# Slab 5 into the bank of the mean square, the first gate slab into bank 6, and the last query slab's mean, root and norm at other places

## The reference, cut to what matters

```
h    = RMSNorm(x)
proj = h @ w_in            # qa ka va | qb kb vb | gate_a gate_b
q, k = per-head RMSNorm    # 16 query heads, 8 + 2 key heads, width 64
ya   = block-sparse causal attention (8 heads); yb = sliding window 128 with sinks (8 heads, 2 kv heads)
x    = x + (sigmoid(gate_a) * (ya @ w_branch_a) + sigmoid(gate_b) * (yb @ w_branch_b)) @ w_out
x    = x + relu(RMSNorm(x) @ w1)^2 @ w2
```

## Time and profile before

| | us |
|---|---|
| median of 3 runs | 678.22 (678.0 to 679.57) |
| profiled execution | 676.66 |
| its span, first to last instruction | 674.9 |
| PE busy / weight loads | 668.8 / 553.7 |
| DVE / ACT / POOL busy | 504.8 / 370.2 / 322.9 |

### The profile page before, as it was taken

One profiled execution on the slowest core, in us unless ns is written; L12 is line 12 of the kernel. 1 busy time (PEld: TensorE's weight loads), 2 busy tenths in 40 slices (PEclk: granted clock), 3 DMA queues, 4 the chain that ended last, 5 costly groups with the idle time before them and its releaser, 6 DMA issues.

```text
span 674.9 us, 9472 instructions
## 1 busy us (share of the span) xinstructions
PE 668.8 (99%) x3238; PEld 553.7 (82%) x3238; DVE 504.8 (75%) x701; ACT 370.2 (55%) x662; POOL 322.9 (48%) x194
## 2 busy tenths in 40 slices
PE   9999999999999999999999999999999999999998
PEld 7878787788888888888888888888888888888886
DVE  6667898555555555785559879788797888978897
ACT  7467676676665566543347546254463525536360
POOL 0246676456556653444446436246352454435532
PEclk9999999999999999999999999999999999999999
DMA  8222242222232213555222232414132151220303
GB/s 320 95 93 94 76 128 82 78 81 93 96 94 75 71 45 113 157 181 188 82 93 93 100 118 65 153 62 154 64 113 104 62 186 62 93 101 25 125 0 125
DMA packets 22909, 69.87 MB, mean 104 GB/s; under 512 B 2731, under 2 KB 4011, under 8 KB 22876
## 3 DMA queue, kind: packets, MB, share of 16 engines
q1 hardware_dynamic: 22588, 68.92, 30.3%
q10 hardware_dynamic: 288, 0.52, 0.2%
HBM read 67.27 MB, written 2.16 MB: 103 GB/s over the span
## 4 chain that ended last, share of the span: by engine, by line
PE 94%; DVE 2%; ACT 2%; issue 1%; DMA 1%; POOL 0%; SPq 0%; DVEq 0%; ACTq 0%
PE bank L1375 20%; PE bank L1377 20%; PE bank L1376 20%; PE bank L1692 8%; PE bank L1689 8%; PE bank L1691 8%; PE bank L1476 3%; PE bank L1538 2%; PE bank L1525 2%; PE bank L1559 1%; PE bank L1561 1%; DMA store<-x_t 1%; PE bank L1661 1%; DVE store L1010 0%; PE bank L1404 0%
## 5 line engine op out<-in xcount | busy, mean ns | idle before, releaser
L534 POOL TENSOR_TENSOR w_lo<-w_raw,w_hi 128x1024 fp32r<-128x1024 f32 x77 | 190.2, 2474 | 232.7 <-ACT w_hi L624 232.7
L1375 PE MATMUL bank<-qk_hi,w_hi 128*128 128x512 f32 x320 | 125.0, 391 | 0.0
L1377 PE MATMUL bank<-qk_hi,w_lo 128*128 128x512 f32 x320 | 124.5, 389 | 0.0
L1376 PE MATMUL bank<-qk_lo,w_hi 128*128 128x512 f32 x320 | 124.5, 389 | 0.0
L1375 PE MATMUL bank<-x_hi,w_hi 128*128 128x512 f32 x304 | 122.4, 403 | 1.6 <-DVE v_parts L1016 1.1
L1377 PE MATMUL bank<-x_hi,w_lo 128*128 128x512 f32 x304 | 118.8, 391 | 0.0
L1376 PE MATMUL bank<-x_lo,w_hi 128*128 128x512 f32 x304 | 118.4, 389 | 0.0
L624 ACT ACTIVATE w_hi<-w_raw 128x1024 fp32r<-128x1024 f32 x80 | 83.9, 1056 | 59.4 <-PE bank L1377 55.0
L1258 DVE SCALAR_TENSOR_TENSOR store<-bank,softmax,store 128x512 f32<-128x512 f32 x101 | 72.0, 744 | 23.2 <-PE bank L1692 23.1
L1692 PE MATMUL bank<-v_parts,x_lo 128*128 128x512 f32 (+1 forms) x218 | 84.4, 387 | 0.0
L1689 PE MATMUL bank<-v_parts,x_hi 128*128 128x512 f32 (+1 forms) x218 | 84.4, 387 | 0.0
(11 more groups left out here) (165 smaller groups left out, 1213.1 us busy)
## 6 DMA issues: line engine op xcount, KB each, us to landing
w_raw<-slabs SPq DMA_DIRECT2D x80, 512.0 KB, 3.3
bias_m<-slabs SPq DMA_DIRECT2D x16, 512.0 KB, 3.6
qk_hi_again<-slabs SPq DMA_DIRECT2D x16, 512.0 KB, 5.2
store<-x_t SPq DMA_DIRECT2D x16, 256.0 KB, 3.4
bias_m<-tab_dram SPq DMA_DIRECT2D x8, 256.0 KB, 4.3
out<-store SPq DMA_DIRECT2D x7, 256.0 KB, 2.1
bias_m<-tab_dram SPq DMA_DIRECT2D x8, 128.0 KB, 3.6
w_raw<-slabs ACTq DMA_DIRECT2D x2, 256.0 KB, 3.4
```

The costliest lines, as they stand in the source:

```text
L534: pool.tensor_tensor(w_lo[:, g % WS, :], w_raw[:, g % RAW, :], w_hi[:, g % WS, :].bitcast(F32), ALU.subtract).then_inc(w_lo_ready, 1)
L1375: pe.matmul(out_, wh, xh, start=first, stop=False)
L1376: pe.matmul(out_, wh, xl, start=False, stop=False)
L1377: last = pe.matmul(out_, wl, xh, start=False, stop=end)
```

## The change: two banks, and the order of the last query slab's norm

- `acc(5)` becomes bank 5, which was the mean square's; PE's wait before slab 5 is `ms_ready` in place of the read of slab 0. Slab 10, in bank 0, now waits for slab 0's read, and the first table product (bank 5) for slab 5's.
- The first gate slab goes to bank 6 and waits for slab 13's read; the second, in bank 0, waits for slab 15's. The transposes of unit 1, which use bank 6, wait for the first gate scale.
- The head sum of slab 16 stands behind kt 5 of slab 17 instead of kt 6.
- On DVE the mean of slab 16 stands ahead of the norm of slab 15 instead of behind it; the norm of slab 16 stands behind the maxima of step 0 instead of in step 2 behind the reciprocals of step 1.
- On ACT the root of slab 16 stands ahead of the split of slab 19 instead of at the end of step 1.

```diff
         def acc(g):
-            return bank[(0, 1, 2, 6, 7)[g % 5]]
+            return bank[5 if g == N_VA + 1 else (0, 1, 2, 6, 7)[g % 5]]
+
+        def gate_bank(j):
+            return bank[0 if j else 6]
...
             for g in range(N_VA, N_QKV):
+                if g == LAST_V:
+                    qkv_root(LAST_Q)
                 split_hi(g + 2)
...
                 if 0 < step < STEPS:
                     exps(step)
-                if step == 1:
-                    qkv_root(LAST_Q)
...
                 else:
                     v_scale(g)
+                if g == LAST_Q:
+                    qk_mean(g)
                 if N_VA <= g - 1 < LAST_Q:
                     qk_norm(g - 1)
-                if not is_v(g):
+                if g < LAST_Q:
                     qk_mean(g)
...
-                dve.tensor_tensor(store[:, j, :], bank[0][:, :], r_all[:, :],
+                dve.tensor_tensor(store[:, j, :], gate_bank(j)[:, :], r_all[:, :],
                                   ALU.mult).then_inc(acc_read, 1)
...
-                if step == 2:
-                    qk_norm(LAST_Q)
                 for e in range(2):
                     if step >= 2:
                         probs_t_lo(*units(step - 2)[e])
                     if step < STEPS:
                         scores_max(*units(step)[e])
+                    if step == 0 and e == 1:
+                        qk_norm(LAST_Q)
...
                     pe.wait_ge(tabw_lo_ready, 1)
-                    pe.wait_ge(ms_ready, 1)
+                    qkv_read(N_VA + 1)
...
-            AFTER[LAST_V, 6] = LAST_Q
+            AFTER[LAST_V, 5] = LAST_Q
             for g in range(N_VA, N_QKV):
                 pe.wait_ge(w_lo_ready, g)
-                if g >= 5:
-                    qkv_read(g - 5)
+                if g == N_VA + 1:
+                    pe.wait_ge(ms_ready, 1)
+                elif g > N_VA + 1:
+                    qkv_read(0 if g == 10 else g - 5)
...
                         pe.wait_ge(pt_lo_ready, u - 1)
+                    if u == 1:
+                        pe.wait_ge(acc_read, read(G_GATE))
...
-                    if j:
+                    if j > 1:
                         pe.wait_ge(acc_read, read(g - 1))
                     else:
-                        qkv_read(g - 3)
-                last = slab_part(g, bank[0], from_x, kts, kts[0] == 0, stop)
+                        qkv_read(LAST_Q - 1 if j else LAST_Q - 3)
+                last = slab_part(g, gate_bank(j), from_x, kts, kts[0] == 0, stop)
```

## The result

| | before | after |
|---|---|---|
| median of 22 runs each | 677.18 us (676.07 to 679.57) | 679.28 us (677.02 to 682.41) |
| profiled execution's span | 674.9 us | 677.0 us |
| mean granted clock in it | 1.000 | 0.997 |

The ratio is 1.0032, 95% interval 1.002 to 1.0044: slower by 2.1 us, just past the 0.3% that a measurement tells from no change. The median of before over 22 runs is 1.0 us lower than that of the three runs that the forecast was built on.

A forecast was written before the change was run, and what follows sets the result against it. TensorE bounds the kernel, busy 668.8 of 674.9 us. Terms -0.54 -0.45 +2.69 -0.49 give +1.2 us: profiled 677.9, and 1.56 above that a median of 679.4 us; 8-in-10 range 677.1 to 680.9.

The forecast's parts named there:

- Slab 5: Slab 5 in bank 5 no longer waits for line 1016: gain 0.54 of 1.28 us, 0.74 returning at line 1403.
- Head sum, mean, maxima: Last query slab's head sum one kt sooner costs 0 to 0.1 us; mean before slab 15's norm costs nothing, maxima at 115.97.
- The gate slab: First gate slab in bank 6 waits for slab 13, not slab 15's norm: gain 0.45 us (0.3 to 0.5).
- The root on ACT and what it drags on POOL: Earlier root delays slab 19's split 1.15 us, itself hidden; POOL's line 534 moves to 116.38, 542 ends at 118.75.
- the race: POOL's line 534 starts 0.48 us ahead of DVE's 984; had POOL lost, v_lo at 122.9 and sum +0.7.
- The norm on DVE: Norm behind step 0's maxima waits for POOL's 534 and 542 in turn; v_lo_ready at 123.40, PE's new stall 2.69 us.
- the first rival: DVE's follow-up 987 goes ahead of POOL's queued 542: stall 1.71 us, sum +0.2, 678.4 us; chance 0.17.
- The gap: PE's new stall before step 2's scores, waiting for v_split_lo: 2.69 us, bounds 0 and 3.4.
- The second rival: Norm instructions cost only their median or lone times: no stall, sum -1.5, 676.7 us, or stall 0.6, sum -0.9; chance 0.12.
- The third stall: PE's second transposes, kept back at line 1111 by the norm in step 2, no longer wait: gain 0.49 us (0 to 0.5).
- The sum: Total of the terms, -0.54 -0.45 +2.69 -0.49 = +1.2 us; profiled execution 677.9 us, median 679.4 us.
- the third rival: PE's gap before step 2's scores sets the granted clock back: 1.3 us more, sum +2.5, 680.7 us; chance 0.11.

The follow-up runs named there:

- e2: The change with POOL's low part of slab 15 moved behind the normalising of step 0: 676.59 us against 677.41 for the kernel before, ratio 0.9994.
- e3: The change with POOL's low parts of slabs 19 and 15 both moved behind the normalising of step 0: 676.55 us against 677.41 before, ratio 0.9985.
- e9: The change with POOL's low part of slab 19 computed twice, one behind the other: 682.13 us against 677.36 for the kernel before, ratio 1.0063.
- e0: The changed kernel itself timed again beside the experiments, its profiled execution at full clock: 679.15 us against 677.41 for the kernel before, ratio 1.0028.
- e4: Both bank changes alone, with mean, root and norm of slab 16 as before: 676.64 us against 677.44 for the kernel before, ratio 0.9987.
- e5: Mean, root and norm at their new places, both banks as before: 679.47 us against 677.44 for the kernel before, ratio 1.0029.

## Why the prediction was right or wrong

**Slab 5** was right: 0.5 us of new idle at line 1403 (1409 now), on the squares' low part, as named, and a gain of 0.56 us where 0.54 was forecast.

**Head sum, mean, maxima**: right. No wait at the sum; the maxima of step 0 came at 114.94 and 115.34 with the norm of slab 15 short (0.69 and 0.69).

**The gate slab**: right in mechanism, too large in size. It starts 0.20 us after the last scores and waits for nothing, but the gain is 0.28 to 0.29 us instead of 0.45, just outside the bounds of 0.3 to 0.5.

**The root on ACT and what it drags on POOL**: right. ACT's split let POOL's 538 start 0.41 us ahead of line 988, where 0.48 was forecast; the race was not lost.

**The norm on DVE**: right in mechanism and size. Forecast were 2.5 and 1.7 us for its first two instructions; 2.54 and 1.67 were measured. The order POOL, DVE, POOL, DVE, which the 0.85 us of the earlier trace rows had suggested and on which the first rival hung, held. The gap was forecast at 2.69 us of PE's order and is 2.48. Of the 0.21, 0.04 lie in the way from line 1046 to PE, for which the earlier trace rows gave 2.32+0.15 and the trace after 2.22+0.21; some 0.15 lie in PE's arrival, later by what the gate slab gained less. The gate slab's error and this one nearly cancel each other in the sum. e2, e3 and e9 take away one POOL instruction, both, or add one, and the norm follows each time. The second rival is refuted by the trace after; e3 shows the condition that it needed, a POOL at rest, with 0.69 us for each. The Trainium skill ("SBUF — State Buffer", section "Who interferes with whom") has the rule that such instructions shut each other out whole and don't share. Every one of these rows agrees: 0.54 to 0.55 us after POOL's end, each time.

**The third stall**: right. The transposes of step 3 wait for nothing; from the scores of step 2 to the late split, e0 is 0.59 us quicker than before, where 0.49 was forecast.

**The sum** was +1.2 us. Between the traces of before and e0, at full clock in both, it is +1.04 (-0.55 -0.29 +2.48 -0.59). The medians of the executions at full clock can't confirm it so closely: 0.3 us over before in the 22 runs, 1.2 in e0. The change as it is came out at +2.1, and the step that failed is the weight of the third rival: I gave the fall of the clock 0.11, since the trace had only a gap of 1.28 us to show. It came in 19 of 34 executions. Its price was about right: 1.3 us forecast from a stretch as long as the gap, 1.6 between the traces with and without the fall (the stretch is longer, some 3.4 us). With forecast and rival at about even odds, the likeliest sum would have been some +2 and the chance of slower by over 0.3% about a half instead of 0.12. That the median, 679.28, lies 0.1 us beside the forecast 679.4 is partly luck: the three runs of before stood 1.0 us above the later median, and this covered the 0.9 us by which the sum was short.

## What to carry to other kernels

Put a VectorE instruction with two SBUF inputs on a path that TensorE waits for only where GpSimd is idle, and look at GpSimd's queue at the new time, not at the old: it was two GpSimd instructions beside it that drew the norm out by 2.8 us. The root's move on ScalarE had put them 1.16 us later (line 538 starts 81.91 us behind the va copies, in e4 80.75), though by these rows they would have met the norm without that as well; no run tests it. Hold a moved step against the latest place that its readers allow as well: here the norm was best behind step 2, where nothing waits for it. And price a new gap of TensorE twice: once for itself, once for the matmuls behind it at the lower clock.

## What the runs showed of the hardware

- The granted clock fell to 1.2 GHz at PE gaps of 1.7 us in 5 of 12 executions, of 2.4 in 19 of 34, of 3.5 in 6 of 6, and in none of 165 with gaps of up to 1.4. It cost 1.6 us in the profiled one of the change and 2.7 in that of e9; in the three profiled falls (after, e5, e9) the windows view shows 1.00 up to 118 us. In the change it fell 1.25 us behind PE's restart, in e9 while PE still stood idle.
- A blocked VectorE instruction (128x512, two SBUF inputs, 0.69 us alone) ended 0.54 to 0.55 us after GpSimd's in every trace shown here; GpSimd's own next one, queued meanwhile, took 0.46 us longer (1.75 instead of 1.29), and went ahead of VectorE's next, though this followed only 0.03 us behind.
